# A triangular inverse in 64x64 blocks: level products on all four tiles of the array, score products ahead of the level sums

## The reference

```python
a = where(strict, (kb @ k.T) * decay, 0)       # kb = k * b, strictly lower
t_inv = triangular_solve(a + eye, eye)         # unit lower triangular inverse
u, w = t_inv @ (v * b), t_inv @ (kb * exp(g))
qk = where(causal, (q @ k.T) * decay, 0)
# scan over chunks, s is the 128x128 state of the head:
v_new = u - w @ s
o = (q * exp(g)) @ s + qk @ v_new
s = s * exp(g_last) + (k * exp(g_last - g)).T @ v_new
```

## Time and profile before

| | |
|---|---|
| median of 3 runs | 1990.46 us (1989.63 to 1992.21) |
| profiled execution | 1988.44 us |
| span of its trace | 1986.6 us |
| mean granted TensorE clock | 0.982 |
| TensorE busy | 1869.2 us (94%) |
| VectorE, ScalarE, GpSimd busy | 964.9, 845.1, 87.9 us |

### The profile page before, as it was taken

How to read it: one execution, slowest core, us unless ns; L and a number is a source line. 1 busy time by engine, 2 the same in 40 slices (tenths; PEclk the granted TensorE clock), 3 DMA queues, 4 the chain that set the end, 5 groups by cost and what they waited for, 6 DMA issues and landing times.

```text
span 1986.6 us, 35678 instructions
## 1 busy us (share of the span) xinstructions
PE 1869.2 (94%) x14484; PEld 1725.9 (87%) x14484; DVE 964.9 (49%) x1558; ACT 845.1 (43%) x1464; POOL 87.9 (4%) x126
## 2 busy tenths in 40 slices
PE   4999999998889999999999999998899999999997
PEld 2999877776779899999999887776798999999997
DVE  4433354445655555325555754344355553255555
ACT  4445322223655544214445644343455442144453
POOL 0000233321000000000000000000000000000000
PEclk8999999999989999999999999999999999999999
DMA  7222454443020122312224311101201223122243
GB/s 276 64 66 57 175 176 168 158 167 115 1 65 25 53 74 78 88 57 74 74 86 132 101 38 48 28 25 43 64 22 56 72 78 88 57 74 74 86 132 112
DMA packets 238715, 170.12 MB, mean 86 GB/s; under 512 B 20138, under 2 KB 230284, under 8 KB 232332
## 3 DMA queue, kind: packets, MB, share of 16 engines
q1 hardware_dynamic: 238604, 168.54, 27.6%
HBM read 165.08 MB, written 3.44 MB: 85 GB/s over the span
## 4 chain that ended last, share of the span: by engine, by line
PE 86%; DVE 5%; ACT 4%; issue 3%; POOL 2%; DMA 0%; SPq 0%; ACTq 0%; DVEq 0%; POOLq 0%
PE ps L1964 48%; PE ps L2040 12%; PE ps L1997 5%; PE ps L2295 4%; PE ps L2145 2%; PE ps L2553 2%; PE ps L2150 2%; PE ps L2590 2%; PE ps L2549 2%; POOL level_b L730 1%; PE ps L2430 1%; PE ps L2407 1%; ACT w_hi L782 1%; PE ps L1985 1%; DVE scores L1762 1%
## 5 line engine op out<-in xcount | busy, mean ns | idle before, releaser
L782 ACT ACTIVATE w_hi<-w_raw 128x1024 fp32r<-128x1024 f32 (+4 forms) x193 | 205.1, 1063 | 580.4 <-PE ps L1964 478.7
L1338 DVE TENSOR_TENSOR w_lo<-w_raw,w_hi 128x1024 fp32r<-128x1024 f32 (+4 forms) x197 | 241.5, 1227 | 394.2 <-ACT w_hi L782 394.0
L1964 PE MATMUL ps<-h_hi,w_hi 128*128 128x322 f32 x1744 | 403.6, 313 | 5.3 <-ACT conv L1169 2.4
L1964 PE MATMUL ps<-h_lo,w_hi 128*128 128x322 f32 x1744 | 402.4, 312 | 0.0
L1964 PE MATMUL ps<-h_hi,w_lo 128*128 128x322 f32 x1744 | 400.1, 310 | 0.0
L1964 PEld LDWEIGHTS ps<-h_hi,w_hi 128*128 128x128 f32 x1744 | 294.2, 189 | 7.2 <-DVE w_lo L1338 3.4
L1964 PEld LDWEIGHTS ps<-h_hi,w_lo 128*128 128x128 f32 x1744 | 295.4, 189 | 0.0
L1964 PEld LDWEIGHTS ps<-h_lo,w_hi 128*128 128x128 f32 x1744 | 295.3, 189 | 0.0
L2040 PE MATMUL ps<-g_hi,w_hi 128*128 128x322 f32 x352 | 110.8, 315 | 2.7 <-DVE g_lo L1810 1.6
L2040 PE MATMUL ps<-g_hi,w_lo 128*128 128x322 f32 x352 | 109.3, 311 | 0.0
L2040 PE MATMUL ps<-g_lo,w_hi 128*128 128x322 f32 x352 | 109.2, 310 | 0.0
(11 more groups left out here) (367 smaller groups left out, 3372.8 us busy)
## 6 DMA issues: line engine op xcount, KB each, us to landing
w_raw<-in_ffn_w_up SPq DMA_DIRECT2D x88, 512.0 KB, 3.6
w_mod_raw<-in_w_mod SPq DMA_DIRECT2D x40, 1024.0 KB, 5.0
w_raw<-in_ffn_w_down SPq DMA_DIRECT2D x48, 704.0 KB, 4.3
w_raw<-in_ev_w_in SPq DMA_DIRECT2D x18, 512.0 KB, 3.6
w_mod_first<-in_w_mod SPq DMA_DIRECT2D x8, 1024.0 KB, 15.7
w_raw<-in_ev_w_out SPq DMA_DIRECT2D x8, 512.0 KB, 3.9
w_raw<-in_od_w_out SPq DMA_DIRECT2D x8, 512.0 KB, 3.8
w_raw<-in_od_w_kv_up SPq DMA_DIRECT2D x24, 128.0 KB, 2.2
```

The lines of the kernel that those rows point to most:

```text
L782: act.activation(WH[slot][:, 0:k, :], RAW[slot][:, 0:k, :], ACT.Copy).then_inc(w_hi, 1)
L1338: dve.tensor_tensor(WL[slot][:, 0:k, :], RAW[slot][:, 0:k, :], WH[slot][:, 0:k, :].bitcast(F32), ALU.subtract).then_inc(w_lo, 1)
L1964: last = pe.matmul(out, w_of(k, wi), x_of(k, xi, i), start=(k == 0 and p == 0), stop=(k == ks - 1 and p == 2))
```

## The change

In the diff, half(b) is the range of 64 partitions of block b, and both(name, c, n) is the n-th count of a semaphore for direction c.

- z of levels 1 to 5 reads partitions of block b and writes those of the other block (crossed_mm): the two off-diagonal tiles. So z, and T with it, lie with their blocks swapped between the halves.
- At level 0 further products with the identity carry B to the other half, into BANK_B, and T starts as I plus that, read from PSUM behind R's start, instead of I + B from SBUF.
- The level sum of R takes T and z from the other half and writes its own half: off-diagonal tiles, into BANK_B. The level sum of T stays on the diagonal tiles and now goes to BANK_C. They alternate head by head.
- z6 and the last product run head by head over both directions, after the waits of both.
- BANK_C still holds the k q scores at level 1, so VectorE's score products stand before the adds of level 1, and TensorE waits for them (qk_ready) before the sums of level 1.
- GpSimd's wait for T's start before level 2 is gone.

```diff
@@ gpsimd: level(lv)
                             pool.wait_ge(*both("z_done", c, LEVELS * r + lv - 1))
-                            if lv == 2:
-                                pool.wait_ge(*both("t_written", c, (LEVELS - 1) * r + 1))
@@ scalar: z_copy(lv)
-                        rows = slice(0, P) if lv < LEVELS - 1 else half(c)
+                        rows = slice(0, P) if lv < LEVELS - 1 else half(1 - c)
@@ vector
                 for c in range(2):
-                    dve.wait_ge(*both("level_ready", c, n0 + 1))
-                    dve.tensor_tensor(TB[c][:, :, :], BS[c][0][:, :, :], ident4, ALU.add).then_inc(S("t_written"), 1)
                     dve.wait_ge(*both("z_done", c, n0 + 1))
                     dve.tensor_tensor(RB[c][:, :, :], b4(bank(BANK_A[c], 256)), ident4, ALU.add).then_inc(S("r_written"), 1)
+                    dve.tensor_tensor(TB[c][:, :, :], b4(bank(BANK_B[c], 256)), ident4, ALU.add).then_inc(S("t_written"), 1)
+                for c in range(2):
+
+                    dve.wait_ge(*both("decay_masked", c, r + 1))
+                    dve.wait_ge(*both("kq_done", c, r + 1))
+                    dve.tensor_tensor(DQ[c][:, :, :], q4(bank(BANK_C[c])), DQ[c][:, :, :], ALU.mult).then_inc(S("qk_ready"), 1)
                 for lv in range(1, LEVELS - 1):
...
-                        dve.tensor_tensor(cols(TB[c], s, c), cols(TB[c], s, c), compact(BANK_B[c], P, s), ALU.add
+                        dve.tensor_tensor(cols(TB[c], s, c), cols(TB[c], s, c), compact(BANK_C[c], 0, s), ALU.add
...
-                            dve.wait_ge(*both("decay_masked", c, r + 1))
-                            dve.wait_ge(*both("kq_done", c, r + 1))
-                            dve.tensor_tensor(DQ[c][:, :, :], q4(bank(BANK_C[c])), DQ[c][:, :, :], ALU.mult
-                                              ).then_inc(S("qk_ready"), 1)
@@ tensor
-                def blocks_mm(out, w, x, h):
+                def crossed_mm(out, w, x, h):
 
                     for b in range(2):
-                        last = pe.matmul(out(b, h), w[half(b), h, :], x(b, h), start=True, stop=True)
+                        last = pe.matmul(out(b, h), w[half(b), h, :], x[half(b), h, :], start=True, stop=True)
                     return last
...
-                        if lv > 0:
+                        if lv == 0:
+                            pe.wait_ge(*both("eg", c, r + 1))
+                        else:
                             pe.wait_ge(*both("r_written", c, n))
...
                         for h in range(4):
-                            last = blocks_mm(lambda b, h: PS[half(b), z0 + B64 * h:z0 + B64 * h + B64], BS[c][lv % 2],
-                                             lambda b, h: level_const(L_ID)[half(b), 0, :] if lv == 0 else RB[c][half(b), h, :], h)
+                            cs = slice(z0 + B64 * h, z0 + B64 * h + B64)
+                            if lv > 0:
+                                last = crossed_mm(lambda b, h: PS[half(1 - b), cs], BS[c][lv % 2], RB[c], h)
+                                continue
+                            for b in range(2):
+                                pe.matmul(PS[half(b), cs], BS[c][0][half(b), h, :], level_const(L_ID)[half(b), 0, :], start=True, stop=True)
+                            last = crossed_mm(lambda b, h: PS[half(1 - b), x0 + B64 * h:x0 + B64 * h + B64], level_const(L_ID), BS[c][0], h)
                         last.then_inc(S("z_done"), 1)
...
                         if lv == 1:
-
-                            pe.wait_ge(*both("eg", c, r + 1))
+                            pe.wait_ge(*both("qk_ready", c, r + 1))
                         for h in range(4):
-                            blocks_mm(lambda b, h: compact1(BANK_B[c], 0, b, h, s), TB[c], lambda b, h: cols1(ZS[c], b, h, s, 1 - c), h)
-                        for h in range(4):
-                            last = blocks_mm(lambda b, h: compact1(BANK_B[c], P, b, h, s), ZS[c], lambda b, h: cols1(TB[c], b, h, s, c), h)
+                            for b in range(2):
+                                pe.matmul(compact1(BANK_B[c], 0, b, h, s), TB[c][half(1 - b), h, :],
+                                          cols1(ZS[c], 1 - b, h, s, 1 - c), start=True, stop=True)
+                            for b in range(2):
+                                last = pe.matmul(compact1(BANK_C[c], 0, b, h, s), ZS[c][half(b), h, :],
+                                                 cols1(TB[c], b, h, s, c), start=True, stop=True)
                         last.then_inc(S("tr_done"), 1)
...
-                    for h in range(4):
-                        last = pe.matmul(PS[half(c), z0 + B64 * h:z0 + B64 * h + B64], BS[c][0][half(1 - c), h, :],
+                for h in range(4):
+                    for c in range(2):
+                        z0 = BANK_A[c] * 512 + B64 * h
+                        last = pe.matmul(PS[half(1 - c), z0:z0 + B64], BS[c][0][half(1 - c), h, :],
                                          RB[c][half(1 - c), h, :], start=True, stop=True)
...
-                    for h in range(4):
-                        last = pe.matmul(PS[half(c), z0 + B64 * h:z0 + B64 * h + B64], TB[c][half(c), h, :],
-                                         ZS[c][half(c), h, :], start=True, stop=True)
-                    last.then_inc(S("tr_done"), 1)
+                for h in range(4):
+                    for c in range(2):
+                        z0 = BANK_B[c] * 512 + B64 * h
+                        last = pe.matmul(PS[half(c), z0:z0 + B64], TB[c][half(1 - c), h, :],
+                                         ZS[c][half(1 - c), h, :], start=True, stop=True)
+                        if h == 3:
+                            last.then_inc(S("tr_done"), 1)
```

## The result

| | before | changed |
|---|---|---|
| median | 1991.34 us (4 runs, 1989.63 to 1994.39) | 1971.62 us (4 runs, 1970.74 to 1975.20) |
| ratio of the times | | 0.9903, 95% interval 0.9885 to 0.9921 |
| profiled execution, span | 1988.44 us, 1986.6 us | 1975.20 us, 1973.4 us |

The change is faster by 19.7 us. I had forecast 24 us (1966.0, range 1957 to 1980): the direction and the range hold, the point is 5.6 us too low. VectorE's list and the score products came out at the size that the sum gave them. The 0.3 us of the last product didn't arrive either.

A forecast was written before the change was run, and what follows sets the result against it. TensorE was taken to bound the kernel (86% of the chain). Terms 2.8 + 1.7 + 0.3 = 4.8 us a round, five rounds 24 us, gave 1964.4 from the profiled 1988.4, forecast as a 1966 us median, range 1957 to 1980.

The forecast's parts named there:

- VectorE's list: Levels 1 and 2: without score products and starting earlier, VectorE reaches the add before z3 1.7 us sooner a round (1.24 to 2.14).
- The 0.3 us of the last product: End of each inverse: interleaved by direction, the last product takes 0.68 instead of 0.96 us, saving 0.3 us a round.
- Four tiles at full pace: Level sums: four tiles run together at 58 ns, 0.47 instead of 0.93 us a direction; forecast case, chance 0.68.
- Levels 3 to 5: Each of these three levels of a round's inverse saves 0.93 us on its sums, 2.8 us a round.
- fed slower: Rival, level sums: four tiles fed only every 21 ns, 0.67 us a direction, 15 us saved, 1975; chance 0.14.
- two at once: Rival, level sums: no more than two tiles run together, sums stay 0.93 us, 1979 to 1985 us; chance 0.07.
- drains: Rival, level sums: changing between off-diagonal and diagonal tiles waits for work under way, some 60 us slower, 2050; chance 0.06.
- no change: Rival, whole inverse: the gain goes into new waits on GpSimd's masks and VectorE's list; chance 0.05.
- What is left of the wait: Before z3: TensorE still idles 1.5 to 2 us, with the clock at half for 3.4 us after it.
- Score products ahead and level 0, nothing: Levels 0 and 1: waiting for earlier score products and the added level-0 instructions were both to cost 0 us.
- 0, with nothing to spare: End of inverse: interleaving z6 delays nothing, ScalarE's copies finishing about when the modulation piece ends and the last product starts.
- If the idle time is gone, 6 us a round: Before z3: if TensorE's idle time disappears, the gain is 6 us a round instead of 4.8.

The follow-up runs named there:

- the second profile: The changed kernel run and profiled again, nothing altered: median 1971.08 us, ratio 0.9895 to the kernel before; profiled span 1966.7 us.
- the bad version: Changed kernel plus 64, 44, 44, 44, 44 unused small products ahead of level 0 by round, placing 256-instruction block edges badly: 1969.82 us, ratio 0.9889.
- the good version: Changed kernel plus 36, 40, 44, 44, 44 unused small products ahead of level 0 by round, placing 256-instruction block edges well: 1963.46 us, ratio 0.9849.
- The kernel with score products ahead alone: Kernel before, with only VectorE's two score products moved ahead of the level-1 adds: 1980.39 us, ratio 0.9942.
- the good, spread version: The good version, with VectorE's direction-1 decay copy and 128x512 product moved from level 1 to behind level 3: 1961.53 us, ratio 0.9843.
- the kernel in turn: Changed kernel, but in each level sum all R products come first and then all T products, instead of alternating: 1974.71 us, ratio 0.9914.
- the spread version: Changed kernel, with VectorE's direction-1 decay copy and 128x512 product moved from level 1 to behind level 3: 1972.80 us, ratio 0.9897.

## Why the prediction was right, and what was mis-sized

- **Four tiles at full pace: right.** 0.47 us a direction, and a level from modulation piece to modulation piece in 3.20 instead of 4.1 us where nothing breaks it. The rivals "fed slower", "two at once", "drains" and "no change" are out by the pace itself and by the measured time.
- **Levels 3 to 5, 2.8 us a round: mis-sized.** This is the largest step that failed. From z3 to the end of the inverse the profile gives -1.2, 2.1, 2.0, 1.9 and 3.8 us by rounds, 8.6 us in all, where the sum had 15.5 (2.8 and 0.3, times five); the second profile gives 12.2. Breaks of 6.3 and 5.1 us lie there. The clock hides in these numbers too: rounds 2 and 3, slow behind z3 as before, gain 2.6 us with their break added back, and the 3.8 us are a round with a break of 0.45 us that no longer has the slow stretch. That breaks cost time is shown by moving them with little else changed: the bad version takes 6.4 us more than the good one for 8.5 us of breaks. By that price the 6.2 to 8.9 us of the changed kernel cost some 3 to 7 us, an estimate, and the forecast missed by 5.6. The sum had looked at what the instructions wait for and how fast the array takes them, and not at where they come from: a level's some 208 instructions now go by in 3.2 us instead of 4.1.
- **VectorE's list, 1.7 us a round: right.** From the level-1 sums to z3 the rounds gain 1.25, 2.16, 1.65, 1.59 and 1.72 us, 1.67 in the mean (1.82 in the second profile). The bounds were 1.24 and 2.14; with its own terms (0.3, 0.3 and 0.32 us off 2.14) the lower one is 1.22.
- **What is left of the wait: right in round 2. Its clock: wrong as a pattern.** 1.8 us of idle time were forecast and 1.75 measured in round 2, with the slow clock; the mean of the five rounds is 1.1 us, 1.2 in the second profile. "The slow 3.4 us of clock stay" came true in two rounds of five, and in one of five of the second profile, where the kernel before had four; a wait of 1.68 us left the clock at 1.00. The forecast took round 2 as the pattern of all five. The kernel with score products ahead alone shows what the forecast had under its "two at once" rival (about 1 us less waiting and the clock kept): 11.5 to 13 us, more than the 1.7 x 5 of the term. The two parts don't simply add up in the changed kernel: with the shorter sums 1.1 to 1.2 us of waiting stand before z3 instead of 0.59.
- **Score products ahead and level 0, nothing: right for the first**, which were ready 1.2 us before the sums of level 1. Level 0 was put at nothing, and the instructions added there do cost nothing at full clock; but the stretch from level 0 to those sums got 4.2 us longer in one profile and 1.5 in the other, by the slow clock. Next to levels 3 to 5 this is the second part of what is missing. Why the clock falls there in one execution and not in another was not settled, nor whether the change makes it likelier.
- **Last products, 0.3 us a round: wrong.** The last product takes 0.68 instead of 0.96 us, as the sum had it, but the 0.28 us don't arrive: from the last level sum to the end of the inverse it is 4.13 to 4.18 us where nothing breaks it, 4.12 before. The step that failed is "0, with nothing to spare": z6 of direction 0 now waits with direction 1's, and the last product starts 0.32 us later behind the sums than before. That is 1.5 us of the forecast's 24.
- **"If the idle time is gone, 6 us a round": right by the round, wrong by the kernel.** Rounds without break or slow clock take 26.0 to 26.2 us (rounds 2 and 3 of the good version, round 4 of the changed kernel's second profile) against 31.9 to 33.5 before, some 6 us; all three still have 1.2 us of idle time before z3, so it is the breaks and the clock that make them, not the idle time. The version without the idle time was no faster, since breaks took its place.

By medians: 13.0 us from the score products, 8 to 9 us from the rest of the change, 19.7 to 21.9 measured. The good version is 7.6 us faster still (1971.1 to 1963.5), by breaks and by the clock at level 0 together; how much each gives was not separated. What starts a fetch is open: in the traces it begins 0.1 to 5 us after TensorE has passed into the block before, often during a modulation piece, and no run varied this by itself.

## What to carry to other kernels

When an edit makes many short instructions go by faster, look in the trace before for breaks called "issue" inside a row of like instructions, count TensorE's records up to them, and set the pace against the fetch: here 208 instructions (loads counted) in 3.2 us met a fetch that was over some 2.3 us after its start. Once they appear, neighbouring edits are worth less than their sum and a few dummy instructions can be worth nearly as much as a real edit (7.6 us here, part of them by the clock); so compare versions only with their blocks in mind. Two parts that shorten the two sides of one wait don't simply add up either: cost them separately and together. And follow a shorter product to the end of its stage: here 0.28 us went into a wait 2 us ahead of it.

## What the runs showed that I had not expected

- TensorE waits for its instructions: breaks at the edge of a block of 256, in packets of 16 KB; the eight of the changed kernel took 0.45 to 1.89 us, the longest in any kernel 2.7 us (round 1 of the good, spread version).
- The queue looks past an instruction whose tile is busy: products for free tiles started 0.2 us before ones ahead of them in the program had started (288.77 in the kernel in turn).
- VectorE's copy of 128x4 takes 0.16 us where no GpSimd operation runs beside it (300.10 us of the spread version), and 0.15 to 1.01 us beside one: 0.31 at 336.07 us of the good version, 1.00 at 342.59 in the changed one. What sets it between the two was not settled.
- The length of a wait did not tell what the clock does behind it: one of 1.58 us before z3 had it at half for 3.4 us, one of 0.59 (score products ahead) and one of 1.68 (round 4 of the changed kernel) left it at 1.00.
